# Encoder layer: latent attention with transposed scores, maxima from a pass of high parts, sums by columns of ones

## What is computed

```python
q = (rmsnorm(c_q) @ w_uq) -> (S, 8, 64 + 32);  q_nope, q_rope = q[..., :64], q[..., 64:]
kv = (rmsnorm(c_kv) @ w_ukv) -> (S, 8, 64 + 64);  k_nope, v = kv[..., :64], kv[..., 64:]
q_rope, k_rope = apply_rope(q_rope), apply_rope(k_rope)   # k_rope (S, 32) is shared by all heads
s = q_nope @ k_nope.T + q_rope @ k_rope.T                 # per head, 512 x 512, float32
p = softmax(s * 96 ** -0.5);  o = p @ v                   # per head, 512 x 64
```

## Time and profile before

| | |
|---|---|
| runs | 1457.08, 1457.85, 1457.98 us; median 1457.85 |
| profiled execution | 1458.1 us, its span 1456.3 us |
| TensorE matmuls | busy 1390.6 us (95%), 6880 |
| VectorE, ScalarE, GpSimd | busy 850.0 (58%), 669.5 (46%), 754.2 us (52%) |
| granted TensorE clock, mean | 0.99 |

### The profile page before, as it was taken

The page is one execution under the profiler, slowest core; times in us unless marked ns, Lnnn a source line. Parts: engine busy times, 40 slices in busy tenths (PEclk is TensorE's granted clock), DMA queues, the critical chain, the costliest instruction groups (busy, mean ns, idle before and its releaser), DMA issues. The chain is left out here.

```text
span 1456.3 us, 19141 instructions
## 1 busy us (share of the span) xinstructions
PE 1390.6 (95%) x6880; PEld 1168.0 (80%) x6880; DVE 850.0 (58%) x1176; ACT 669.5 (46%) x1297; POOL 754.2 (52%) x599
## 2 busy tenths in 40 slices
PE   8998899999999998999999899999999999999998
PEld 6986688887889866898888778888888888888776
DVE  3469933225354697331245977666666665578966
ACT  6437844535425387454453533333223333444355
POOL 4732246831435422577316765555555553466894
PEclk9999999999999999999999999999999999999999
DMA  7420034523322200445126033333322225873334
GB/s 268 148 64 15 0 115 119 180 66 106 100 67 77 72 1 1 145 136 154 44 87 229 18 129 117 109 109 109 109 97 93 95 92 181 309 262 111 85 102 152
DMA packets 98858, 162.82 MB, mean 112 GB/s; under 512 B 8529, under 2 KB 42193, under 8 KB 98769
## 3 DMA queue, kind: packets, MB, share of 16 engines
q1 hardware_dynamic: 98768, 161.65, 34.5%
HBM read 133.04 MB, written 28.57 MB: 111 GB/s over the span
## 5 line engine op out<-in xcount | busy, mean ns | idle before, releaser
L704 POOL TENSOR_TENSOR w_lo<-w_raw,w_hi 128x512 fp32r<-128x512 f32 (+2 forms) x236 | 304.1, 1304 | 288.6 <-ACT w_hi L880 287.6
L880 ACT ACTIVATE w_hi<-w_raw 128x512 fp32r<-128x512 f32 (+2 forms) x236 | 140.4, 605 | 251.2 <-PE ps L1885 243.9
L1883 PE MATMUL ps<-h_hi_P,w_hi 128*128 128x512 f32 x616 | 241.9, 393 | 5.8 <-DVE h_lo_P L1329 3.1
L1884 PE MATMUL ps<-h_lo_P,w_hi 128*128 128x512 f32 x616 | 240.8, 391 | 0.0
L1885 PE MATMUL ps<-h_hi_P,w_lo 128*128 128x512 f32 x616 | 240.7, 391 | 0.0
L704 POOL TENSOR_TENSOR w_lo<-w_sum,w_hi 128x512 fp32r<-128x512 f32 x88 | 118.3, 1348 | 118.2 <-ACT w_hi L880 118.0
L704 POOL TENSOR_TENSOR w_lo<-a_raw,w_hi 128x512 fp32r<-128x512 f32 x77 | 112.0, 1457 | 74.1 <-ACT w_hi L880 74.0
L1883 PE MATMUL ps<-w_hi,act_hi 128*128 128x512 f32 (+1 forms) x384 | 141.2, 368 | 1.6 <-issue 1.6
L1883 PEld LDWEIGHTS ps<-h_hi_P,w_hi 128*128 128x128 f32 x616 | 116.3, 189 | 32.6 <-issue 4.7
L1885 PE MATMUL ps<-w_hi,act_lo 128*128 128x512 f32 (+1 forms) x384 | 140.1, 365 | 0.0
L1884 PE MATMUL ps<-w_lo,act_hi 128*128 128x512 f32 (+1 forms) x384 | 140.1, 365 | 0.0
(11 more groups left out here) (237 smaller groups left out, 3056.7 us busy)
## 6 DMA issues: line engine op xcount, KB each, us to landing
gu_raw<-in_w_gate_up SPq DMA_DIRECT2D x22, 1024.0 KB, 5.4
a_raw<-a_mem SPq DMA_DIRECT2D x77, 256.0 KB, 2.7
w_raw<-in_w_xkv SPq DMA_DIRECT2D x64, 256.0 KB, 3.0
a_mem<-down_sum SPq DMA_DIRECT2D x44, 256.0 KB, 2.6
wd<-in_w_down SPq DMA_DIRECT2D x44, 256.0 KB, 5.7
a_mem<-act_t SPq DMA_DIRECT2D x33, 256.0 KB, 2.1
w_raw<-in_w_out SPq DMA_DIRECT2D x32, 256.0 KB, 2.7
w_raw<-in_w_xq SPq DMA_DIRECT2D x32, 256.0 KB, 2.9
```

The lines of the kernel that those rows point to most:

```text
L704: return nc.gpsimd.tensor_tensor(out, whole, hi.bitcast(F32), ALU.subtract)
L880: return nc.scalar.activation(out, in_, ACT.Copy)
L1883: nc.tensor.matmul(out, s_hi, m_hi, start=start, stop=False, skip_group_check=more)
L1884: nc.tensor.matmul(out, s_hi, m_lo, start=False, stop=False, skip_group_check=more)
```

## The change

The weights of the queries and keys are laid out anew on the host. Queries (`query`), keys (`key_pair`, two heads at a time) come out of the projection transposed: features on the partitions, tokens along the columns. The 32 rotary features of a query are computed twice, as they are and with halves swapped, so that a head fills 128 rows; one multiplication with a table (`turn`: ones, cosines, signed sines) out of PSUM (`query_out`) makes both terms of the rotation, and the key's rotated part stands twice beside `k_nope`, so that the matmul adds the terms. The rotary key is transposed once a group (`key_rope`). The row maxima come from one matmul of high parts for each 128 queries (`row_maxima`, into two banks at a time) instead of from the scores. `head_diag` writes them on the diagonal of a 128x128 tile for each of the four query tiles, and a fourth matmul with a tile of minus ones subtracts them from the scores in PSUM. The scores are made with keys on the partitions (`scores`), so the exponential is at once what the value matmul takes: no transposes of probabilities, no bias, no sum on ScalarE. The value tiles hold 64 columns of ones beside 64 of values (`v_hi_st`; zeros in `v_lo_st`), so the same matmul (`weighted`) gives the sums in the other half of the rows. The division comes last, for two heads together (`pair_recip` in two halves, `pair_scale`). TensorE runs 32 steps (head h, key tile b), in which the queries two heads ahead, the maxima of the next head and the key pairs are interleaved, and the first three steps of `out0` lie in and after the last head. The weights of `out0` are converted during the heads (`EARLY_HI`, `EARLY_LO`). The memory fetch waits for the last `pair_lo`. The order of the ten weight tiles is now v, keys A, q0, keys B, q1.

The diff, cut to its core (in each hunk eight blanks of indentation are left off):

```diff
-     ("q0", T, (w_uq, CQ, 0, QP)),
-     ("kv0", T, (w_ukv, CK, 0, BANK)), ("kv1", T, (w_ukv, CK, BANK, BANK)),
-     ("q1", T, (w_uq, CQ, QP, QP)),
+     ("vv", 16, (w_v, CK, 0, BANK)), ("kA", 0, (w_k, 1, 0, BANK)), ("q0", 0, (w_q, CQ, 0, BANK)),
+     ("kB", 0, (w_k, 1, 0, BANK)), ("q1", 0, (w_q, CQ, BANK, BANK)),
...
+v_hi_st = at("v_hi_st", R + 6, [P, T, PAIRS, 3, DV], F32R)
+v_lo_st = at("v_lo_st", R + 18, [P, T, PAIRS, 3, DV], F32R)
+max_diag = [act[:, PAIRS - 1, :].rearrange("p (t q) -> p t q", q=P) for act in (act_hi, act_lo)]
...
+    def prob_lo(g, n):
+        pool.wait_ge(p_hi.sem, p_hi.at(g, n + 1))
+        sub(pt_lo[:, n % 3, :], prob[:, n % 2, :], pt_hi[:, n % 3, :]).then_inc(p_lo.sem, 1)
+    def pair_lo(g, p):
+        pool.wait_ge(y_hi.sem, y_hi.at(g, p + 1))
+        sub(act_lo[:, p, :], y_n[:, p % 2, :], act_hi[:, p, :]).then_inc(y_lo.sem, 1)
...
+        nc.gpsimd.memset(v_hi_st[:, :, :, 1, :].bitcast(F32), 1.0).then_inc(v_filled.sem, 1)
+        nc.gpsimd.memset(v_lo_st[:, :, :, 1, :].bitcast(F32), 0.0).then_inc(v_filled.sem, 1)
...
+        query_lo(g, 0)
+        EARLY_LO = {(0, 1): ("vv", 0), (0, 3): ("vv", 1), (1, 0): ("kA", 0), (1, 1): ("q0", 0), (1, 3): ("q0", 1),
+                    (2, 1): ("q0", 2), (5, 0): ("kB", 0), (5, 3): ("q1", 0), (6, 1): ("q1", 1), (6, 3): ("q1", 2)}
+        for h in range(HEADS):
+            for b in range(T):
+                if b == 0 and h + 1 < HEADS:
+                    query_lo(g, h + 1)
+                prob_lo(g, T * h + b)
+                if b == 3 and h >= 3 and h % 2 == 1:
+                    pair_lo(g, (h - 3) // 2)
+                if (h, b) in EARLY_LO:
+                    name, k = EARLY_LO[h, b]
+                    weights_lo(g, name, k, k + 1)
+        pair_lo(g, PAIRS - 1)
...
+    def query_hi(g, h):
+        if h >= 2:
+            act.wait_ge(b_full.sem, b_full.at(g, T * (h - 1)))
+        act.wait_ge(*free(g, f"Q{h}"))
+        copy(qt_hi[:, h % 2, :], q_f[:]).then_inc(q_hi.sem, 1)
+    def key_hi(g, h):
+        if h >= 2:
+            act.wait_ge(b_full.sem, b_full.at(g, T * (h - 1)))
+        act.wait_ge(*full(g, f"K{h // 2}"))
+        o = half_rows(h % 2)
+        copy(kt_hi[o, h % 2, :], ps[o, K_BANK, :]).then_inc(k_hi.sem, 1)
+    def value_hi(g, t):
+        act.wait_ge(*full(g, f"v{t}"))
+        copy(v_hi_st[:, t, :, 0:3:2, :],
+             ps[:, V_BANK[t], :].rearrange("p (q j d) -> p q j d", j=2, d=DV)).then_inc(hi_done.sem, 1)
+    def prob_out(g, n):
+        act.wait_ge(b_full.sem, b_full.at(g, n + 1))
+        if n >= 2:
+            act.wait_ge(p_lo.sem, p_lo.at(g, n - 1))
+        nc.scalar.activation(prob[:, n % 2, :], ps[:, B_BANK[n % 2], :], ACT.Exp,
+                             scale=scale).then_inc(p_exp.sem, 1)
+        act.wait_ge(p_exp.sem, p_exp.at(g, n + 1))
+        if n >= 3:
+            act.wait_ge(v_done.sem, v_done.at(g, n - 2))
+        copy(pt_hi[:, n % 3, :], prob[:, n % 2, :]).then_inc(p_hi.sem, 1)
+    def sums_out(g, h):
+        act.wait_ge(v_done.sem, v_done.at(g, T * (h + 1)))
+        if h >= 4:
+            act.wait_ge(y_lo.sem, y_lo.at(g, h // 2 - 1))
+        copy(y_n[half_rows(h % 2), h // 2 % 2, :], ps[half_rows(1 - h % 2), Y_BANK[h % 2], :]).then_inc(y_sums.sem, 1)
+    def pair_hi(g, p):
+        act.wait_ge(y_scaled.sem, y_scaled.at(g, p + 1))
+        copy(act_hi[:, p, :], y_n[:, p % 2, :]).then_inc(y_hi.sem, 1)
...
+        key_rope_hi(g)
+        query_hi(g, 0)
+        key_hi(g, 0)
+        key_hi(g, 1)
+        act.wait_ge(v_filled.sem, v_filled.at(g, 2))
+        for t in range(T):
+            value_hi(g, t)
+        for h in range(HEADS):
+            for b in range(T):
+                if b == 0 and h + 1 < HEADS:
+                    query_hi(g, h + 1)
+                    if h >= 1:
+                        key_hi(g, h + 1)
+                prob_out(g, T * h + b)
+                if b == 2 and h >= 1:
+                    sums_out(g, h - 1)
+                if b == 2 and h >= 3 and h % 2 == 1:
+                    pair_hi(g, (h - 3) // 2)
+                if (h, b) in EARLY_HI:
+                    name, k = EARLY_HI[h, b]
+                    weights_hi(g, name, k, k + 1)
+        sums_out(g, HEADS - 1)
+        pair_hi(g, PAIRS - 1)
...
+    def query_out(g, h):
+        dve.wait_ge(*full(g, f"Q{h}"))
+        if h >= 1:
+            dve.wait_ge(q_lo.sem, q_lo.at(g, h))
+        nc.vector.tensor_tensor(q_f[:], ps[:, Q_BANK, :], turn[:, h % 2, :], ALU.mult).then_inc(psum_free.sem, 1)
+    def key_lo(g, h):
+        dve.wait_ge(k_hi.sem, k_hi.at(g, max(h + 1, 2)))
+        o = half_rows(h % 2)
+        sub(kt_lo[o, h % 2, :], ps[o, K_BANK, :],
+            kt_hi[o, h % 2, :]).then_inc(k_lo.sem if h % 2 == 0 else psum_free.sem, 1)
+    def value_lo(g, t):
+        dve.wait_ge(hi_done.sem, hi_done.at(g, HI["vv"] + t + 1))
+        sub(v_lo_st[:, t, :, 0:3:2, :], ps[:, V_BANK[t], :].rearrange("p (q j d) -> p q j d", j=2, d=DV),
+            v_hi_st[:, t, :, 0:3:2, :]).then_inc(psum_free.sem, 1)
+    def head_max(g, h, half):
+        o = h % 2 * T + 2 * half
+        dve.wait_ge(a_full.sem, a_full.at(g, 2 * h + half + 1))
+        nc.vector.tensor_reduce(rowmax[:, o:o + 2], ps[:, A_BANK:A_BANK + 2, :], AX.X,
+                                ALU.max).then_inc(a_max.sem, 1)
+    def head_diag(g, h):
+        dve.wait_ge(a_max.sem, a_max.at(g, 2 * h + 2))
+        if h >= 2:
+            dve.wait_ge(b_full.sem, b_full.at(g, T * (h - 1)))
+        o = h % 2 * T
+        nc.vector.tensor_tensor(max_diag[h % 2], ident[:].unsqueeze(1).broadcast_to([P, T, P]),
+                                rowmax[:, o:o + T].unsqueeze(2).broadcast_to([P, T, P]),
+                                ALU.mult).then_inc(diag.sem, 1)
+    def values_out(g, h):
+        dve.wait_ge(y_sums.sem, y_sums.at(g, h + 1))
+        if h >= 2:
+            dve.wait_ge(y_scaled.sem, y_scaled.at(g, h // 2))
+        o = half_rows(h % 2)
+        nc.vector.tensor_copy(y_raw[o, :], ps[o, Y_BANK[h % 2], :]).then_inc(y_copied.sem, 1)
+    def pair_recip(g, p, half):
+        dve.wait_ge(y_sums.sem, y_sums.at(g, 2 * p + 2))
+        o = y_n[:, p % 2, half * S // 2:(half + 1) * S // 2]
+        nc.vector.reciprocal(o, o).then_inc(y_recip.sem, 1)
+    def pair_scale(g, p):
+        dve.wait_ge(y_recip.sem, y_recip.at(g, 2 * p + 2))
+        dve.wait_ge(y_copied.sem, y_copied.at(g, 2 * p + 2))
+        nc.vector.tensor_tensor(y_n[:, p % 2, :], y_raw[:], y_n[:, p % 2, :], ALU.mult).then_inc(y_scaled.sem, 1)
...
+        dve.wait_ge(turn_in, 16 * (g + 1))
+        query_out(g, 0)
+        key_rope_lo(g, 0)
+        key_rope_lo(g, 1)
+        key_lo(g, 0)
+        head_max(g, 0, 0)
+        key_lo(g, 1)
+        value_lo(g, 0)
+        head_max(g, 0, 1)
+        head_diag(g, 0)
+        for t in range(1, T):
+            value_lo(g, t)
+        query_out(g, 1)
+        for h in range(HEADS):
+            if h >= 3 and h % 2 == 1:
+                pair_recip(g, (h - 3) // 2, 1)
+            if h >= 1 and h + 1 < HEADS:
+                key_lo(g, h + 1)
+            if h >= 3 and h % 2 == 1:
+                pair_scale(g, (h - 3) // 2)
+            if h + 1 < HEADS:
+                head_max(g, h + 1, 0)
+                head_max(g, h + 1, 1)
+                head_diag(g, h + 1)
+            if h >= 1:
+                values_out(g, h - 1)
+            if h + 2 < HEADS:
+                query_out(g, h + 2)
+            if h >= 2 and h % 2 == 0:
+                pair_recip(g, (h - 2) // 2, 0)
+        values_out(g, HEADS - 1)
+        for half in range(2):
+            pair_recip(g, PAIRS - 1, half)
+        pair_scale(g, PAIRS - 1)
...
+    def query(g, h, k):
+        w = W["q0" if h < PAIRS else "q1"] + k
+        pe.wait_ge(w_ready.sem, w_ready.at(g, w + 1))
+        if k == 0 and h > 0:
+            pe.wait_ge(*free(g, f"Q{h - 1}"))
+        if h == 0:
+            pe.wait_ge(psum_free.sem, psum_free.at(g, TEN["c"] + k + 1))
+        o = slice(h % PAIRS * P, (h % PAIRS + 1) * P)
+        last = three(ps[:, Q_BANK, :], w_hi[:, w % RING, o], w_lo[:, w % RING, o], c_hi[:, k, :], c_lo[:, k, :],
+                     k == 0, k == CQ - 1)
+        if k == CQ - 1:
+            last.then_inc(psum_full.sem, 1)
+        elif h % PAIRS == PAIRS - 1:
+            last.then_inc(w_used.sem, 1)
...
+    def row_maxima(g, h, half):
+        pe.wait_ge(q_hi.sem, q_hi.at(g, h + 1))
+        pe.wait_ge(k_hi.sem, k_hi.at(g, h + 1))
+        if h == 0 and half == 0:
+            pe.wait_ge(kr_lo.sem, kr_lo.at(g, 2))
+            pe.wait_ge(psum_free.sem, psum_free.at(g, FB[2] + 1))
+        if h > 0 or half > 0:
+            pe.wait_ge(a_max.sem, a_max.at(g, 2 * h + half))
+        for i in range(2):
+            t = 2 * half + i
+            last = nc.tensor.matmul(ps[:, A_BANK + i, :], qt_hi[:, h % 2, t * P:(t + 1) * P], kt_hi[:, h % 2, :],
+                                    start=True, stop=True)
+        last.then_inc(a_full.sem, 1)
```

(81 more changed lines are left out.)

464 lines of the change are left out of this document (145 added, 319 removed).

## The result

The changed kernel takes 1438.24 us (median of 4 runs, 1436.78 to 1439.31) against 1457.91 of the kernel before, run beside it (4 runs, 1457.08 to 1460.79): a ratio of 0.9861, 95% interval 0.9844 to 0.9878. It gives 19.7 us where 9.9 were forecast. The profiled execution took 1438.64 us, its span 1436.9 (before: 1458.1 and 1456.3).

What follows compares the result with a forecast made beforehand. TensorE's sequence sets the end, the old loop paced by VectorE and ScalarE handing on. Per group 116.2 work + 7.0 waits + 4 tail = 127.2 against 132.1 us, saving 9.8 in all: 1448 us; eight in ten from 1433 to 1458.

Steps and rivals of the forecast that it cites:

- TensorE's work: Whole stage, per group: matmuls through three steps of `out0`, plus twenty transposes, take 116.2 us if nothing waits.
- heads 6 and 7: End of the head loop: no queries to fill with, GpSimd's seven operations outlast head 6's matmuls; 0.7 to 1.0 us lost.
- `out0`'s seventh tile: After the last head: GpSimd makes this weight tile after `pair_lo`, TensorE has only 8.3 us of work; 1.8 us lost.
- memory rows: Memory transposes: the fetch starts at 8.8 instead of 3.6 us, so normalised rows come late; about 2 us lost.
- VectorE in the loop: Head loop: VectorE's work is 15.7 to 17.8 us a pair against TensorE's 20.2; it binds by order, not sum.
- the waits of heads 3 and 5: Second maxima pass waits while reciprocals, `key_lo` and `pair_scale` precede VectorE's first maximum: 0.4 to 1.8 us a head.
- The 1452 of that sentence: Head loop: whole time if the skill's exclusive port lock made odd heads' `head_diag` dearer, losing 1.8 us more a group.
- The covers holding: Rival, head loop and tail: reciprocals cost only 0.35 us, so other work hides them; 119.7 us a group, 1433; chance 0.22.
- the mixed case of 124.2: Covers hold partly: cheap two-input operations but 2.3 us reciprocals; 124.2 us a group, 1442 whole; no separate chance given.
- The slow clock's case: Rival, head loop: waits lower TensorE's clock, two drops a group at 2.3 us each; 1457, no change; chance 0.12.
- That case's 1462: Rival, head loop: GpSimd sets the pace at 1.74 us an operation; 134 us a group, slower at 1462; chance 0.12.
- It doesn't do what it says: Rival, whole change: maxima of high parts or sums by ones might need extra steps; no size or separate chance given.

Runs made afterwards that it cites:

- Experiment 1: Changed kernel with two extra VectorE reciprocals of 24 columns ahead of each half reciprocal: 1443.68 us, ratio 0.9896 to the kernel before.
- Experiment 10: Kernel before with 12 useless matmuls filling TensorE's 2.9 us idle time ahead of head 1's scores: 1458.08 us against 1459.62, ratio 0.9988.
- experiments 5 and 8: Changed kernel: first, weight tiles of (6,1), (6,3) moved to head 7, 1437.25 us; second, also (5,3)'s and `out0`'s seventh tile moved, memory fetched early, 1432.47 us.
- experiment 9: Kernel before with the scaling of probabilities by the reciprocal sums left out: 1456.73 us against 1458.92, ratio 0.9987.
- experiment 4: Changed kernel with two extra GpSimd operations of 24 columns ahead of each `prob_lo`: 1451.82 us, ratio 0.9957 to the kernel before.

## Why the forecast fell short, step by step

The direction and the mechanism of the gain were right. Its size was half of what came. Per group, from the first matmul behind the c transposes to the end of the memory transposes, in us:

| step of the prediction | forecast | group 0 | group 1 |
|---|---|---|---|
| TensorE's work | 116.2 | 114.7 | 114.7 |
| opening | 1.0 | 0.9 | 0.7 |
| heads 0 to 5 with restarts | 5.1 | 1.4 | 1.4 |
| heads 6 and 7 | 0.9 | 3.0 | 3.1 |
| `out0`'s seventh tile | 1.8 | 1.0 | 1.0 |
| memory rows | 2 | 1.3 | 0.7 |
| sum | 127.2 | 122.4 | 121.6 |

(The rows below the first are the lost time, rounded, and the first is what is left; the forecast's 5.1 is its 7.0 less the opening and the middle of 0.7 to 1.0 for heads 6 and 7. Its tail of 1.8 and 2 was rounded up to 4, so its rows add up to 127.0.) The same stretch of the kernel before took 132.1 and 131.6, so it is 9.7 and 10.1 shorter; in group 0 the c transposes take 0.5 more, since the clock rose later.

**The step that failed is "VectorE in the loop", its term for the two reciprocals**, and with it the waits of heads 3 and 5. I took 2.3 us for a 128x256 reciprocal, from the slope of two rows of 2 and 8 columns. It takes 1.72. VectorE's timeline in head 3 of the kernel after, and TensorE's pass of high parts that it was to hold up:

```profile
130.04 3.35 DVE L1431 RECIPROCAL y_n<-y_n 128x256 f32<-128x256 f32 x2
133.31 0.62 DVE L1344 TENSOR_TENSOR kt_lo<-ps,kt_hi 64x512 fp32r<-64x512 f32 x1
133.86 0.67 DVE L1436 TENSOR_TENSOR y_n<-y_raw,y_n 128x512 f32<-128x512 f32 x1
134.45 1.21 DVE L1409 TENSOR_REDUCE stats<-ps 128x2 f32<-128x1024 f32 x1
```
```profile
129.40 0.39 PE L2071 MATMUL ps<-qt_hi,kt_hi 128*128 128x512 f32 x1
...
131.73 0.39 PE L2071 MATMUL ps<-qt_hi,kt_hi 128*128 128x512 f32 x1
...
134.45 0.39 PE L2071 MATMUL ps<-qt_hi,kt_hi 128*128 128x512 f32 x1
...
136.04 0.61 PE L2051 MATMUL ps<-kt_hi,qt_hi 128*128 128x512 f32 x2
```

The four groups of VectorE operations are through at 135.66, 6.26 us after the scores start at 129.40 (forecast 7.0 to 8.4); TensorE comes at 6.64 (forecast 6.65). The margin is 0.4 us; the 1.16 us by which I had taken the two reciprocals too dear would turn it into a wait. TensorE's side was right to a hundredth. VectorE's was off by the reciprocals, and `pair_scale` came at the cheap end of its two prices (0.67, of 0.68 and 1.40). The forecast's low end of 7.0 doesn't follow from its own parts either: 6.0 and 1.22 are 7.2. Experiment 1 puts back most of the forecast's size, and 5.4 us return, over half of the 9.8 that were missing.

Of the 3.7 us that heads 0 to 5 came out cheaper a group, 2.2 were forecast for this wait (the middle of 0.4 to 1.8, twice). The rest is the diagonals (1.05 forecast, 0.5 measured), the next head's first query (1.0 and 0.4) and the restarts (0.8 and 0.5).

Two bounds stood in the text, 0.35 and 2.4, and I took 2.3 because "two reciprocal rows show the slope". The slope of 9 ns a column was read between 0.158 and 0.212 us, a difference of 54 ns on operations that are mostly a fixed cost, and stretched forty times. (1721 - 158) / 254 is 6.2 ns a column.

**TensorE's work.** 496 matmuls at 0.23 are 114.1; I had used 0.69 for a triple, read between 91.75 and 92.44, which is rounded up. Twelve matmuls from 131.73 to 134.45 give 0.2267. Over 496 matmuls that is 1.6 us a group, 3 us in all: a pace that multiplies a large count must be read over a long row, not over one pair.

**Opening.** Forecast 1.0, measured 0.9 and 0.7, of which 0.6 at `query(2)` behind `query_out(1)`, where it was put.

**Diagonals and the next query.** `head_diag` was to make 0 to 0.7 in odd heads, the first query after it 0.5 in heads 2 and 4. Measured are 0.12 to 0.26 (with the restart behind it 0.2 to 0.35) and 0.20. The groups of VectorE by shape:

```profile
L1409 DVE TENSOR_REDUCE stats<-ps 128x2 f32<-128x1024 f32 x32 | 39.1, 1222 | 37.0 <-PE ps L2051 36.8
L1431 DVE RECIPROCAL y_n<-y_n 128x256 f32<-128x256 f32 x16 | 26.9, 1721 | 0.1
...
L1417 DVE TENSOR_TENSOR act_lo<-ident,stats 128x512 fp32r<-128x512 f32 x8 | 8.5, 1068 | 0.3
...
L1417 DVE TENSOR_TENSOR act_hi<-ident,stats 128x512 fp32r<-128x512 f32 x8 | 6.3, 793 | 0.3
```

The even heads' diagonals, on which TensorE waits, take 0.79 on the mean and the odd ones' 1.07, the longest of all 1.468. This is a little more than the 1.40 that the earlier trace rows had as their largest, and 0.5 less than the 1.99 of the estimate. The Trainium skill's rule (SBUF — State Buffer, "SBUF: two separate sides") is thus not contradicted by the trace and not shown by it: no diagonal paid a whole instruction of GpSimd, and none of them held TensorE for more than 0.3. The 1452 of that sentence did not come.

**ScalarE, and the slow clock.** Right: no wait of TensorE is for an exponential, and the clock is 1.00 in the loop, even after head 6's wait of 1.7. That it stayed up has some luck in it: in experiment 1 it fell behind the same wait, 1.8 us there, in both groups. Experiment 10 shows that the prediction overrated what the slow clock had cost the old kernel; this changed no term, since the sum was made from the new work upward.

**Heads 6 and 7.** Here I was too low: 3.0 against 0.9, which hid 2.1 us a group of the other terms' error. I had counted the seven operations inside head 6, and missed that `pair_lo`, the tile of (5,3) and `query_lo(7)` delay its first `prob_lo` (experiments 5 and 8).

**Tail.** 1.0 for the tile against 1.8, which is the reciprocals again: twice 0.58 is more than the difference. The memory rows 1.3 and 0.7 against 2. What the later fetch costs was right in kind, and gone when the fetch goes early.

**What bounds the kernel now** was read wrongly in one sentence. "The loop goes at the pace of VectorE and ScalarE handing tiles on" was half true: the load did not bound it (experiment 9), and by its waits the handing on did. Busy shares of 50.7 and 48.2 us in 56.2 looked like a bound and were not one.

**Rivals.** The covers holding comes nearest in kind: its 119.7 a group for cheap reciprocals (0.35) lies 1.9 to 2.7 under what came, and most of the difference is heads 6 and 7. The truth lay between it and the mixed case of 124.2. The slow clock's case did not come in the kernel after, but its condition was near (experiment 1); where the clock did fall in head 6 it took back less than the 2.3 us a drop that the case counts, since the next wait got shorter. GpSimd's `prob_lo` took 1.29 us by the median (mean 1.36), under 1.45; with 1.74 a step for `prob_lo` alone, experiment 4, the kernel is still 6 us faster than before. That case's 1462 had 1.74 for all 54 operations, which no run tried. "It doesn't do what it says" is out: the 496 matmuls and 20 transposes that the prediction counted make 114.5 us at 0.2267 and 0.104, and the trace has 114.7.

## What to carry to other kernels

A cost for a shape that the trace doesn't have is not to be had by stretching a slope between two small operations. Where two ends are as far apart as 0.35 and 2.4 us, write down at which value the wait appears (here about 1.9 a reciprocal, from the margin of 0.4 us for two), and put the chances on the two sides of it. And where a list feeds a bottleneck, don't sum per iteration: write out what stands ahead of the first item that is needed.

Busy shares of 90% on two engines don't prove that they bound a loop. Take load away and see whether the period moves: here 8.8 us less on VectorE moved a head from 9.46 to 9.42 us. The waits then say where the hand-overs are.

And the price of a slow clock is not that of the slow matmuls. What stands behind it may have waited anyway, so compare the length of the stage.
